# Dilated attention by units of two heads: 64-row score products, 64-column output products, the row sum folded into the head norm

## The chip, the cores and the metric

The kernel is one program on one core of a Trainium2 chip. The metric is the device time of one execution in microseconds. TensorE, VectorE, ScalarE and GpSimd each run their own list of instructions and meet through semaphores; SyncE and GpSimd issue the DMAs.

## The reference

Three model blocks follow each other on a sequence of 1024 tokens with 1024 channels, all in float32. Only the attention of the third block is touched by the change:

```python
q = rms_norm(q.reshape(B, S, 8, 64), q_norm_g) * 64 ** -0.5
k = rms_norm(k.reshape(B, S, 8, 64), k_norm_g)
for window, dilation in ((128, 1), (512, 4), (2048, 16)):
    num, m, den = dilated_band(q, k, v, slopes, window, dilation)   # softmax parts of one band, with an ALiBi bias
attn = sum(exp(m_i - max) * num_i) / sum(exp(m_i - max) * den_i)
attn = rms_norm(attn, attn_out_g.reshape(8, 64))                     # over the 64 channels of a head
```

The kernel computes the three bands as one causal attention: a key that several bands hold gets the logarithm of their count added to its bias, a key that none holds gets -1e30. So for one head the work is: scores of 1024 queries against the keys up to them, plus a bias table, row maximum, exp, row sum, product with the values, division, and an RMS norm over the head's 64 channels.

## The kernel before

Activations lie transposed: a tile is 128 channels x 1024 tokens, so one tile of `A` holds two heads, head e=0 on partitions 0 to 63 and e=1 on 64 to 127. There are four such pairs; `A[:, pair]` is q, `A[:, pair + 4]` is k, `B[:, pair]` is v. The stage lies between the linear layer `qkv3` and the linear layer `rwl`. GpSimd clears `X` and copies each head's q rows into a tile of its own with zeros in the other 64 rows (`q_staged`, L2318 to L2323), while `qkv3` still runs; with these a score product over all 128 rows gives one head's scores.

One step of the loop is one head and one block of 128 queries: 64 steps (`BLOCKS_3`), 16 for a pair, e=0 first. Within a head the blocks go 7, 0, 6, 1, 5, 2, 4, 3; block b meets b + 1 blocks of 128 keys. A float32 product is two matrix instructions, each with its own weight load; a float32 transpose is one.

For step g the engines do, each in the order given, with `g+2` the step ahead and `g-1` the one behind:

- TensorE: scores of g+2 (L2482, weights the 128 queries, moving the keys, at most 512 at a time), the b + 1 transposes of g (L2490), the output of g-1 (L2501: weights 128 keys x 128 queries of weights, moving 128 keys x 64 channels, b + 1 of them accumulated).
- VectorE: score plus bias with the row maximum out of PSUM (L3017, `tensor_tensor_reduce`, up to 1024 wide), the negation of the maximum (L3021), the copy of the transposed rows of g out of PSUM (L3028), the reciprocal of the row sum (L3030).
- ScalarE: exp of g+2 with its row sum (L2832), the copy of the output of g-1 scaled by the reciprocal (L2839).

Once a pair: two halves of v transposed into tokens x channels (TensorE L2464, ScalarE L2809); for the finished pair squares (ScalarE L2814), their sum (VectorE L2999), square root (ScalarE L2818, with a table load, and another load for the next exp), reciprocal and scaling (VectorE L3003, L3006), and the transposes back to channels x tokens (TensorE L2464, ScalarE L2822). Scores have two places in PSUM (banks 0 and 1 for the wide blocks, bank 2 for the others), the transposes two (4 and 5, and 7), the output one (bank 6). The bias tables of two heads at a time lie in `kept`, loaded by GpSimd's queue (L2327).

After the stage, `rwl` (L183) runs its 64 instructions at once, in the order of tiles and halves (0,0), (1,0), (0,1), (1,1), with the last pair's transposes between them. GpSimd then saves the attention's result (L2329) and loads `pair_const` (L2331); VectorE waits for that load (L3091) before it evacuates `rwl`'s banks (L3043, L3045), which the next layer's products wait for.

Of the kernel before, what the change touches and what calls it, by code (L numbers as in the profile page):

```python
# [18 lines left out]
P = 128  # L19
# [73 lines left out]
def build(nc, io, out):  # L93

    with ExitStack() as ctx:
# [2005 lines left out]
        if 3 in BLOCKS:  # L2101
# [4 lines left out]
            bias_landed = [sem(f"bias_landed{e}") for e in range(2)]  # L2106
# [4 lines left out]
            qk_dve = steps("qk_vector", "recip " + " ".join(f"scaled{m}" for m in range(DT)))  # L2111

            BLOCK_ORDER = [7, 0, 6, 1, 5, 2, 4, 3]
            BLOCKS_3 = [(pair, e, b) for pair in range(4) for e in range(2) for b in BLOCK_ORDER]
            NB = len(BLOCKS_3)
            VTURN_AT = {16 * (pair - 1) + at: (pair, half) for pair in range(1, 4) for half, at in ((0, 10), (1, 12))}
            OTURN_AT = {16 * (pair + 1) + at: (pair, half) for pair in range(3) for half, at in ((0, 6), (1, 8))}
            OSQ_AT, OSUM_AT, OSTD_AT, OSCALE_AT = ({16 * (pair + 1) + at: pair for pair in range(3)} for at in (1, 2, 3, 4))

            def along(first, last, extras, *kinds):  # L2120

                names = [first]
                for g in range(-2, NB + 1):
                    names += [f"{kind}{g + lag}" for kind, lag in kinds if 0 <= g + lag < NB]
                    for table, made in extras:
                        if g in table:
                            names.append(made(table[g]))
                return " ".join(names + [last])
            half_name = lambda kind: lambda at: f"{kind}{at[0]}_{at[1]}"
            named = lambda *kinds: lambda pair: " ".join(f"{kind}{pair}" for kind in kinds)  # L2130
            dil_pool = steps("dilated_gpsimd", " ".join(f"low{pair} high{pair}" for pair in range(4)))
            dil_pe = steps("dilated_tensor", along("vturn0_0 vturn0_1", "oturn3_0 oturn3_1",
                                                   [(VTURN_AT, half_name("vturn")), (OTURN_AT, half_name("oturn"))],
                                                   ("s", 2), ("turn", 0), ("o", -1)))
            dil_act = steps("dilated_scalar", along("vtok0_0 vtok0_1", "osq3 ostd3 oout3_0 oout3_1",
                                                    [(OSQ_AT, named("osq")), (OSTD_AT, named("ostd")), (VTURN_AT, half_name("vtok")),
                                                     (OTURN_AT, half_name("oout"))], ("exp", 2), ("on", -1)))
            dil_dve = steps("dilated_vector", along("", "osum3 orstd3 oscale3",
                                                    [(OSUM_AT, named("osum")), (OSCALE_AT, named("orstd", "oscale"))],
                                                    ("max", 2), ("neg", 2), ("pt", 0), ("recip", 0)))  # L2140
            dil_zero = steps("dilated_zero", "zeroed")

            q_staged = lambda pair, e: X[:, 2 * pair + e, :]
            v_heads = [C[:, 7, :].rearrange("p (s n) -> p s n", s=NT), B[:, 4, :].rearrange("p (s n) -> p s n", s=NT)]
            o_heads = [B[:, 5, :], B[:, 6, :]]
            o_room = norm_sums.rearrange("p w j t -> p (w j t)")[:, 0:SEQ]
            small_rows = C[:, 6, :].rearrange("p (n t) -> p n t", n=2)
            p_rows = lambda g: small_rows[:, g // 2 % 2, :] if g % 2 else C[:, 4 + g // 2 % 2, :]
            p_cols = lambda g: B[:, 7, 0:HALF] if g % 2 else C[:, 3, :]
            score_bank = lambda g: bank[:, 2, :] if g % 2 else pair_banks(0)  # L2150
            turn_rows = lambda g: bank[:, 7, :] if g % 2 else pair_banks(4)
            out_cols = lambda g: bank[:, 6, 0:64]
            head_sum = kept[:, 0:8 * P].rearrange("p (m r) -> p m r", m=8)
            head_spread = kept[:, 8 * P:16 * P].rearrange("p (m r) -> p m r", m=8)
            row_max, row_neg, row_sum3, row_recip3 = (cols[:, 4 * n:4 * n + 4] for n in range(4))
            o_sum, o_std, o_rstd = (cols[:, 16 * n:16 * n + 16] for n in (1, 2, 3))
# [154 lines left out]
        def b3_gpsimd(pool):  # L2311
# [4 lines left out]
            pool.memset(X[:, :, :], 0.0).then_inc(*dil_zero.did("zeroed"))  # L2316
            pool.wait_ge(*dil_zero.all())
            for pair in range(4):  # L2318
                pool.wait_ge(*qk_dve.after(0, f"scaled{pair}"))
                for e, name in enumerate(("low", "high")):  # L2320
                    rows = slice(64 * e, 64 * e + 64)
                    nc.gpsimd.tensor_copy(q_staged(pair, e)[rows], A[rows, pair, :]).then_inc(*dil_pool.did(f"{name}{pair}"))
                    pool.wait_ge(*dil_pool.after(0, f"{name}{pair}"))  # L2323
            for pair in range(4):
                for e in range(2):
                    pool.wait_ge(*(dil_dve.after(0, f"max{16 * (pair - 1) + 8 * e + 7}") if pair else qk_pe.after(0, "spread7")))
                    pool.dma_start(kept[:, e * SEQ:(e + 1) * SEQ], io["dilated_bias"][2 * pair + e]).then_inc(bias_landed[e], 16)  # L2327
# [1181 lines left out]
```

## Time and profile before

| | us |
|---|---|
| median of 3 runs | 4563.32 |
| the runs | 4549.02, 4565.37, 4563.32 |
| span of the profiled execution | 4563.6 |
| TensorE busy in it | 4427.4 (97%) |
| VectorE, ScalarE, GpSimd busy | 1772.2, 900.7, 852.0 |
| dilated stage, 2784.1 to 2989.06 | 204.96 |

The times shown don't mark which run was profiled; its span lies 0.3 us above their median, and that span is taken as its own time too. The stage is found by the first transposes of v (L2464) at 2784.14 us and the first instruction of `rwl` at 2989.06 us. Busy time of a matrix instruction includes its run through the array after its last column went in, so instructions in a row overlap in the record; the pace of a run of them is read from start to start or from the chain of waits.

### The profile page before, as it was taken

What the parts mean: (1) busy time and instruction counts of PE and PEld (TensorE: products, weight loads), DVE (VectorE), ACT (ScalarE), POOL (GpSimd) and SP (SyncE); (2) the same over time, 40 slices, a digit from 0 to 9 for tenths busy, and PEclk for the clock granted to TensorE, in tenths of its full rate; (3) what the DMA queues carried; (4) which work ended last, traced back from release to release, by engine and by line L of the source; (5) the groups of instructions that cost most, each with busy time, mean ns of one, the idle gap of its engine ahead of it and who ended that gap; (6) DMA issues with size and microseconds to landing.
All of it is one profiled execution on the core that took longest, in us unless ns stands there. A gap on an engine that the chain in (4) does not pass through costs nothing.

```text
span 4563.6 us, 37880 instructions
## 1 busy us (share of the span) xinstructions
PE 4427.4 (97%) x15188; PEld 2387.4 (52%) x15188; DVE 1772.2 (39%) x2821; ACT 900.7 (20%) x1603; POOL 852.0 (19%) x656
## 2 busy tenths in 40 slices
PE   8999999999999999999999999899999999999999
PEld 4467444444444456654444445644699744444444
DVE  4635463333325123333996403534333332222311
ACT  2114120000002122221332112431244310000000
POOL 5212042423201100000552000000111003222310
PEclk9989999999999999999999999999999999999999
DMA  4420101111111110001111111010000121111121
GB/s 188 157 82 1 37 28 37 46 46 46 37 46 65 37 72 12 10 19 37 37 37 46 56 46 37 19 49 28 14 1 1 56 92 42 41 46 46 66 75 44
DMA packets 52605, 215.45 MB, mean 47 GB/s; under 512 B 5856, under 2 KB 7392, under 8 KB 50512
## 3 DMA queue, kind: packets, MB, share of 16 engines
q1 hardware_dynamic: 47808, 168.58, 10.5%
q0 software_dynamic: 4624, 44.45, 2.5%
q8 instruction: 122, 2.00, 0.2%
q14 instruction: 51, 0.42, 0.0%
HBM read 194.13 MB, written 18.87 MB: 47 GB/s over the span
## 4 chain that ended last, share of the span: by engine, by line
PE 91%; DVE 4%; POOL 1%; ACT 1%; issue 1%; DMA 1%; SPq 0%; DVEq 0%; POOLq 0%; ACTq 0%
PE bank L474 30%; PE bank L183 28%; PE bank L2554 7%; PE bank L2741 4%; PE bank L1700 2%; PE bank L1753 2%; PE bank L2752 1%; PE bank L1736 1%; PE bank L2482 1%; PE bank L1739 1%; PE bank L2501 1%; PE bank L2581 1%; PE bank L1716 1%; PE bank L2730 1%; PE bank L2682 1%
## 5 line engine op out<-in xcount | busy, mean ns | idle before, releaser
L183 PE MATMUL bank<-H,ring 128*128 128x512 f32 x1920 | 835.2, 596 | 10.6 <-ACT H L371 4.7
L183 PEld LDWEIGHTS bank<-H,ring 128*128 128x128 f32 x1920 | 366.1, 191 | 469.9 <-issue 454.2
L183 PE MATMUL bank<-ABC,ring 128*128 128x512 f32 x1200 | 520.1, 594 | 2.5 <-POOL ABC L1654 2.0
L183 PEld LDWEIGHTS bank<-ABC,ring 128*128 128x128 f32 x1200 | 226.7, 190 | 286.4 <-issue 278.0
L474 PE MATMUL bank<-H,ring 128*128 128x512 f32 x736 | 323.5, 593 | 0.8 <-ACT ABC L1799 0.8
L2067 DVE SCALAR_TENSOR_TENSOR bank<-ABC,params,bank 128x1024 f32<-128x1024 f32 x184 | 237.3, 1290 | 8.0
L474 PEld LDWEIGHTS bank<-H,ring 128*128 128x128 f32 x736 | 140.0, 190 | 176.9 <-issue 176.9
L474 PE MATMUL bank<-H,X 128*128 128x512 f32 x400 | 179.9, 593 | 0.4 <-POOL H L825 0.4
L474 PE MATMUL bank<-X 128*128 128x512 f32 x400 | 179.8, 593 | 0.0
L474 PE MATMUL bank<-X,ring 128*128 128x512 f32 x368 | 165.4, 593 | 0.0
L1639 POOL TENSOR_TENSOR ABC<-ABC 128x1024 f32<-128x1024 f32 x48 | 113.3, 2361 | 220.4 <-ACT ABC L1873 214.4
L1186 ACT ACTIVATE norm_room<-bank 128x512 f32<-128x512 f32 x27 | 16.1, 597 | 612.7 <-PE bank L474 612.7
L474 PEld LDWEIGHTS bank<-H,X 128*128 128x128 f32 x400 | 76.0, 190 | 96.3 <-issue 94.6
L474 PEld LDWEIGHTS bank<-X 128*128 128x128 f32 x400 | 76.1, 190 | 95.5 <-issue 95.3
L474 PE MATMUL bank<-ABC,ring 128*128 128x512 f32 x288 | 126.1, 593 | 0.0
L461 POOL TENSOR_TENSOR X<-ring 128x512 f32<-128x512 f32 x31 | 39.9, 1286 | 457.2 <-DMA ring<-in_gu 185.8
L474 PEld LDWEIGHTS bank<-X,ring 128*128 128x128 f32 x368 | 70.0, 190 | 87.9 <-issue 87.9
L3151 DVE COPY_PREDICATED ring<-kept,bank 128x512 f32<-128x512 int32 x80 | 56.5, 724 | 151.9 <-PE bank L2554 151.9
L1993 DVE CUSTOM_DVE_ANT_0 H<-bank,kept 128x1024 f32<-128x1024 f32 (+3 forms) x64 | 48.3, 754 | 170.3 <-PE bank L1739 170.3
L1489 DVE SCALAR_TENSOR_TENSOR ABC<-bank,params,norm_room 128x512 f32<-128x512 f32 x60 | 45.1, 751 | 171.2 <-PE bank L474 171.2
L2345 POOL COPY X<-ABC 64x256 f32<-64x256 f32 x128 | 50.6, 396 | 294.4 <-PE bank L2581 266.1
L2554 PE MATMUL bank<-ring,H 128*128 128x128 f32 x720 | 97.9, 284 | 3.8 <-DVE H L3171 2.1
(548 smaller groups left out, 6780.8 us busy)
## 6 DMA issues: line engine op xcount, KB each, us to landing
ABC<-in_ada SPq DMA_DIRECT2D x48, 512.0 KB, 5.7
ring<-in_gu SPq DMA_DIRECT2D x44, 512.0 KB, 4.2
ring<-in_up SPq DMA_DIRECT2D x32, 512.0 KB, 4.0
ring<-in_down SPq DMA_DIRECT2D x32, 512.0 KB, 4.1
ring<-in_conv_in SPq DMA_DIRECT2D x24, 512.0 KB, 4.2
ring<-in_ffn SPq DMA_DIRECT2D x16, 704.0 KB, 5.3
ring<-in_proj SPq DMA_DIRECT2D x16, 512.0 KB, 5.9
ring<-in_mix SPq DMA_DIRECT2D x16, 512.0 KB, 4.4
```

Source lines behind the costliest of these rows:

```text
L183: mm = nc.tensor.matmul(bank[:, 2 * (m % 2) + h, :], ring[:, s % RING, k * P:(k + 1) * P], rhs(k)[:, h * HALF:(h + 1) * HALF], start=(k == ...
L474: mm = nc.tensor.matmul(S.bank(j, slot), lhs[:, k * P:(k + 1) * P], rhs[:, k, :], start=start and k == 0, stop=(k == 3), skip_group_check= ...
L1639: nc.gpsimd.tensor_tensor(C[:, c, :], C[:, c, :], conv_parts[k % 2], ALU.add).then_inc(*conv_pool.did(f"tap{k}"))
L1700: mm = nc.tensor.matmul(bank[:, b + h, :], w(first + k), A[:, src + k, h * HALF:(h + 1) * HALF], start=(k == 0), stop=(k == n - 1))
L1716: mm = nc.tensor.matmul(bank[:, 6 + c // 4, (c % 4) * P:(c % 4 + 1) * P], A[:, 3 + k, c * P:(c + 1) * P], w(5 + k), start=(k == 0), stop=( ...
L1753: mm = nc.tensor.matmul(bank[:, 6, 0:P], p_turned(n)[:, k * P:(k + 1) * P], v_tok[:, k, :], start=(k == 0), stop=(k == LENGTHS[n]))
L1993: nc.vector.tensor_tensor_reduce(p_exp(n)[:, 0:(b + 1) * P], score_bank(n)[:, 0:(b + 1) * P], causal_row[:, (NT - 1 - b) * P:], 1.0, -3e38 ...
L2067: nc.vector.scalar_tensor_tensor(conv_rows(c), conv_us[c % 4][:, k:k + SEQ], conv_tap(c, k), conv_rows(c), ALU.mult, ALU.add).then_inc(*co ...
L2345: last = nc.gpsimd.tensor_copy(dst[rows, :, block], src[rows, :, chunk3(c)])
L2554: mm = nc.tensor.matmul(bank[:, b, at + q * width:at + q * width + width], lhs[:, q, :], rhs(q), start=start and (q == 0 or stop), stop=st ...
L2741: mm = nc.tensor.matmul(bank[:, down_bank[b], :], lhs[:, k * P:(k + 1) * P], rhs[:, k, :], start=start and k == 0, stop=stop and k == 7, s ...
L3151: nc.vector.copy_predicated(x_lev[n], mask_i(n, 0), bank_q(2 if n < 3 else 3)).then_inc(*rw_dve.did(f"x{n}_{c}"))
```

## The change

The loop now goes over 32 units of one pair and one block, both heads together. Scores are two products over 64 rows each (`A[rows, ...]` with rows 0 to 63 and 64 to 127), into two banks, so GpSimd's clearing and copying of q is gone. A unit with more than four key blocks is worked in two parts of at most 512 keys. The q spread constants and the bias table are negated on the host: scores come out negated, VectorE takes a minimum with the running value of the first part, and exp runs with scale -1 and the minimum as bias, so no negation is left. The output product is turned: weights are 64 columns of v (128 keys x 64 channels), moving are the transposed rows, and the two heads write partitions 0 to 63 and 64 to 127 of one bank, channels x queries already. Nothing is divided by the row sum: with n the unscaled output and s the row sum, the norm of n/s is n / sqrt(mean(n*n) + eps*s*s). For that ScalarE squares the output of each unit, TensorE takes the mean by a product with the two columns of `one_head` (eight products of 2 columns a pair), and 16 products (weights a broadcast column, moving the identity) spread the reciprocal root back over 64 partitions each; VectorE scales. The copy of the transposed rows is split: head 0 by VectorE, head 1 by ScalarE.

In a step ScalarE does the copy of part 0 of unit g, the copy and the squares of the output of g-1, the copy of part 1, the two exps of g+2, and in the step after a pair's mean product the square root. VectorE does the variance or the reciprocal of the finished pair where due, the two minima of part 0 of g+2, the copy of part 0 of g, the minima of part 1, the copy of part 1, and the scaling where due. The reciprocal is the first thing of VectorE's step 3 behind a pair, the spread products the last of TensorE's steps 3 and 5.

```diff
@@ schedule
-            BLOCKS_3 = [(pair, e, b) for pair in range(4) for e in range(2) for b in BLOCK_ORDER]
+            UNITS = [(pair, b) for pair in range(4) for b in BLOCK_ORDER]
+            parts_of = lambda n: [(a, min((UNITS[n][1] + 1) * P, a + HALF)) for a in range(0, (UNITS[n][1] + 1) * P, HALF)]
+            behind = lambda at: {8 * (pair + 1) + at: pair for pair in range(3)}
+            MS_AT, VAR_AT, RECIP_AT, SPREAD0_AT, SCALE0_AT, SPREAD1_AT, SCALE1_AT = (behind(at) for at in (1, 2, 3, 3, 4, 5, 5))
+            VTURN_AT = {8 * (pair - 1) + 6 + half: (pair, half) for pair in range(1, 4) for half in range(2)}
+            bias_rows = [kept.rearrange("p (e t) -> p e t", e=2), C[:, 4:6, :]]
+            dilated_bank = lambda n, i, e: bank[:, 2 * ((PART_AT[n] + i) % 2) + e, :]
+            out_rows = bank[:, 7, 0:P]
+            mean_squares = bank[:, 6, 0:16]
@@ GpSimd
-            pool.memset(X[:, :, :], 0.0).then_inc(*dil_zero.did("zeroed"))
...
-                    nc.gpsimd.tensor_copy(q_staged(pair, e)[rows], A[rows, pair, :]).then_inc(*dil_pool.did(f"{name}{pair}"))
...
-            pool.wait_ge(*dil_act.all())
+            pool.wait_ge(*dil_dve.all())
             pool.dma_start(attention_kept, C[:, 0:4, :]).then_inc(mix_spilled, 16)
@@ TensorE
+            def scores(n, i):
...
+                    pe.wait_ge(*dil_dve.after(0, f"max{m}_{before - PART_AT[m]}_1"))
+                a, z = parts_of(n)[i]
+                for e in range(2):
+                    rows = slice(64 * e, 64 * e + 64)
+                    mm = nc.tensor.matmul(dilated_bank(n, i, e)[:, 0:z - a], A[rows, pair, b * P:(b + 1) * P], A[rows, pair + 4, a:z],
+                                          start=True, stop=True)
+            def rows_turned(n, i):
...
+                for e, copied in enumerate((dil_dve, dil_act)):
+                    if i == 0:
+                        pe.wait_ge(*dil_act.after(0, f"exp{n}_{e}"))
+                    if i:
+                        pe.wait_ge(*copied.after(0, f"pt{n}_{i - 1}"))
...
+                    for at in range(a, z, P):
+                        mm = nc.tensor.transpose(bank[:, 4 + e, at - a:at - a + P], p_rows(n, e)[:, at:at + P], ident[:, :])
+            def heads_out(n):
...
+                pe.wait_ge(*dil_dve.after(0, f"pt{n}_{last}"))
+                pe.wait_ge(*dil_act.after(0, f"pt{n}_{last}"))
+                if n:
+                    pe.wait_ge(*dil_act.after(0, f"square{n - 1}"))
+                for k in range(b + 1):
+                    for e in range(2):
+                        rows = slice(64 * e, 64 * e + 64)
+                        mm = nc.tensor.matmul(out_rows[rows], v_heads[pair % 2][:, k, rows], p_cols(n, e)[:, k * P:(k + 1) * P],
+                                              start=(k == 0), stop=(k == b), skip_group_check=True)
+            def heads_mean(pair):
...
+                for b in range(NT):
+                    mm = nc.tensor.matmul(mean_squares[:, 2 * b:2 * b + 2], out_squares[pair % 2][:, b * P:(b + 1) * P], one_head,
+                                          start=True, stop=True, skip_group_check=True)
+            def heads_spread(pair, half, b):
+                pe.wait_ge(*dil_dve.after(0, f"recip{pair}"))
+                for n in range(4):
+                    for e in range(2):
+                        at = 2 * (4 * half + n) + e
+                        mm = nc.tensor.matmul(bank[64 * e:64 * e + 64, b, n * P:(n + 1) * P], o_rstd[:, at:at + 1].broadcast_to([P, 64]),
+                                              ident[:, :], start=True, stop=True, skip_group_check=True)
+            for g in range(-2, NU + 1):
+                if g + 2 < NU:
+                    scores(g + 2, 0)
+                if 0 <= g < NU:
+                    rows_turned(g, 0)
+                if g + 2 < NU:
+                    scores(g + 2, 1)
+                if 0 <= g - 1:
+                    heads_out(g - 1)
+                if 0 <= g < NU:
+                    rows_turned(g, 1)
...
+            linear(pe, "rwl", lambda k: H[:, k, :], between={(1, 0, 0): lambda: heads_mean(3), (0, 1, 4): lambda: heads_spread(3, 0, 4),
+                                                            (0, 1, 5): lambda: heads_spread(3, 1, 5)})
@@ ScalarE
+                nc.scalar.activation(p_cols(n, 1)[:, a:z], bank[:, 5, 0:z - a], ACT.Identity).then_inc(*dil_act.did(f"pt{n}_{i}"))
+                nc.scalar.activation(C[:, pair, now], out_rows, ACT.Identity).then_inc(*dil_act.did(f"kept{n}"))
+                nc.scalar.activation(out_squares[pair % 2][:, now], out_rows, ACT.Square).then_inc(*dil_act.did(f"square{n}"))
+                    nc.scalar.activation(rows, rows, ACT.Exp, scale=-1.0, bias=row_min(n, e, last),
+                                         accum_out=row_sums(pair)[:, 2 * b + e:2 * b + e + 1]).then_inc(*dil_act.did(f"exp{n}_{e}"))
@@ VectorE
+                    nc.vector.tensor_tensor_reduce(p_rows(n, e)[:, a:z], dilated_bank(n, i, e)[:, 0:z - a], bias_rows[pair % 2][:, e, at + a:at + z],
+                                                   1.0, row_min(n, e, 0) if i else 3e38, ALU.add, ALU.min, row_min(n, e, i)
+                nc.vector.tensor_copy(p_cols(n, 0)[:, a:z], bank[:, 4, 0:z - a]).then_inc(*dil_dve.did(f"pt{n}_{i}"))
+                nc.vector.tensor_tensor(o_twice, row_sums(pair), row_sums(pair), ALU.mult).then_inc(*dil_dve.did(f"twice{pair}"))
+                nc.vector.scalar_tensor_tensor(o_twice, o_twice, eps_rms, mean_squares, ALU.mult, ALU.add).then_inc(*dil_dve.did(f"var{pair}"))
+                v.wait_ge(*dil_act.after(0, f"std{pair}"))
+                nc.vector.reciprocal(o_rstd, o_std).then_inc(*dil_dve.did(f"recip{pair}"))
+                nc.vector.scalar_tensor_tensor(rows, rows, par("attn_out_g", pair), bank[:, b, :], ALU.mult, ALU.mult
@@ host
-                head_const[2 * m + e, 8 + m, rows] = 0.125 if m < 4 else 1.0
+                head_const[2 * m + e, 8 + m, rows] = -0.125 if m < 4 else 1.0
-        arrays["dilated_bias"] = bias.astype(np.float32)
+        arrays["dilated_bias"] = (-bias).astype(np.float32)
```

## Rows read from the trace of the kernel before

**Rows 1.** Busy time by engine: the dilated stage, then its second pair.

```profile
core 0: us, PE busy (x) PEld busy (x) DVE busy (x) ACT busy (x) POOL busy (x), PEclk, DMA share, GB/s
...
2784.10:2989.06 204.96, 182.84 (x1112) 138.98 (x1113) 112.36 (x329) 90.90 (x220) 3.17 (x6) 0.94 0.07 21
...
2836.00:2887.00 51.00, 45.79 (x280) 34.63 (x279) 28.65 (x83) 23.48 (x56) 1.05 (x2) 0.93 0.07 21
```

**Rows 2.** Waits in 2785 to 3000 us: waiter, releaser, total us, times, longest.

```profile
DVE ABC L3017 <- PE bank L2482: 105.5, 35, 22.9
ACT ABC L2832 <- DVE cols L3021: 90.0, 47, 4.7
```

**Rows 3.** Chain that ended last, pieces in the stage: start, us, what.

```profile
2825.95 0.65 PE bank L2490 x6
...
2829.92 1.79 PE bank L2482 x4
...
2836.34 3.10 PE bank L2482 x4
...
2842.22 1.97 PE bank L2501 x16
...
2850.55 1.28 ACT L2818
```

**Rows 4.** Groups by line and form, 2780 to 3010 us: TensorE's products.

```profile
L2501 PE MATMUL bank<-ABC 128*128 128x64 f32 x576 | 74.4, 275 | 20.3 <-ACT ABC L2839 17.1 <-DVE cols L3030 1.4 <-DVE ABC L3028 1.1
...
L2482 PE MATMUL bank<-ABC,X 128*128 128x512 f32 x96 | 58.0, 706 | 1.3 <-DVE cols L3017 1.3
```

**Rows 5.** The same view: VectorE and ScalarE, widest and narrowest forms.

```profile
L2839 ACT ACTIVATE ABC<-bank,cols 128x64 f32<-128x64 f32 x64 | 19.3, 302 | 22.9 <-PE bank L2501 22.9
...
L3017 DVE CUSTOM_DVE_ANT_0 ABC<-bank,kept 128x1024 f32<-128x1024 f32 x8 | 9.8, 1225 | 43.4 <-PE bank L2482 43.4
...
L3028 DVE COPY ABC<-bank 128x1024 f32<-128x1024 f32 x8 | 9.8, 1224 | 0.0
...
L2832 ACT ACTIVATE ABC<-ABC,cols 128x1024 f32<-128x1024 f32 x8 | 9.2, 1148 | 27.2 <-DVE cols L3021 27.2
...
L2809 ACT ACTIVATE ABC<-bank 128x512 f32<-128x512 f32 x8 | 4.6, 586 | 0.8 <-PE bank L2464 0.8
...
L2832 ACT ACTIVATE ABC<-ABC,cols 128x128 f32<-128x128 f32 x8 | 3.1, 391 | 0.0
L3028 DVE COPY ABC<-bank 128x128 f32<-128x128 f32 x8 | 2.3, 291 | 0.0
L3017 DVE CUSTOM_DVE_ANT_0 ABC<-bank,kept 128x128 f32<-128x128 f32 x8 | 2.2, 273 | 0.0
```

**Rows 6.** Timeline of TensorE in an earlier stage: start, us, line, tile*form.

```profile
380.50 1.02 PE L964 MATMUL bank<-kept,ident 128*128 128x512 f32 x2
381.45 1.16 PE L967 MATMUL bank<-ABC,kept 64*128 64x128 f32 x8
382.44 0.61 PE L972 MATMUL bank<-ABC,kept 64*128 64x128 f32 x4
382.98 0.66 PE L977 MATMUL bank<-ident,ABC 128*128 128x128 f32 x4
```

**Rows 7.** Windows of 2 us within the stage, columns as Rows 1.

```profile
2834.00:2836.00 2.00, 1.12 (x10) 1.15 (x10) 1.11 (x7) 1.12 (x5) 0.00 (x0) 0.97 0.00 0
2836.00:2838.00 2.00, 2.00 (x5) 0.96 (x5) 0.00 (x0) 0.31 (x1) 0.00 (x0) 0.50 0.00 0
```

**Rows 8.** Timeline after the stage: start, us, engine, line, idle before.

```profile
2989.06 15.67 PE L183 MATMUL bank<-H,ring 128*128 128x512 f32 x32 [0.45 <-ACT ABC L2839]
...
3010.59 0.53 POOL L2331 DMA_DIRECT2D kept<-in_pair_const  x1
...
3019.03 0.88 DVE L3091 TENSOR_SCALAR ring<-kept,params 128x128 f32<-128x128 f32 x4 [24.58 <-DMA kept<-in_pair_const]
...
3021.43 8.82 PE L183 MATMUL bank<-H,ring 128*128 128x512 f32 x20 [2.09 <-DVE ABC L3045]
```

More of the change, by code:

```diff
@@ L2117, in build @@
[L2117 to L2134, printed above, removed]
@@ new lines, in part, with unit, extra @@
+            def part(kind, lag, i, *ends):
+                return lambda g: [f"{kind}{g + lag}_{i}{end}" for end in ends or ("",) if 0 <= g + lag < NU and i < len(parts_of(g + lag))]
+            def unit(lag, *kinds):
+                return lambda g: [kind.format(g + lag) for kind in kinds if 0 <= g + lag < NU]
+            def extra(table, *kinds):
+                return lambda g: [kind.format(table[g]) for kind in kinds if g in table]
+            turned_v = lambda g: [f"vturn{VTURN_AT[g][0]}_{VTURN_AT[g][1]}"] if g in VTURN_AT else []
@@ new lines, in heads_spread @@
+            def heads_spread(pair, half, b):
[5 more added lines that the diff above has]
+                                              ident[:, :], start=True, stop=True, skip_group_check=True)
+                mm.then_inc(*dil_pe.did(f"spread{pair}_{half}"))
@@ L2514, in b3_tensor @@
-            pe.wait_ge(*last_in_bank3)
-            pe.wait_ge(*dil_act.after(0, f"on{NB - 1}"))
-            linear(pe, "rwl", lambda k: H[:, k, :], between={(0, 1, 0): lambda: out_turned(3, 0, 4), (0, 1, 4): lambda: out_turned(3, 1, 5)})
+                    if half:
+                        pe.wait_ge(*dil_act.after(0, f"vtok{pair}_0"))
+                    elif pair >= 2:
+                        pe.wait_ge(*dil_dve.after(0, f"scale{pair - 2}_1"))
+                    else:
+                        pe.wait_ge(*dil_act.after(0, "vtok0_0"))
@@ new lines, in weights @@
+            def weights(n):
+                pair, b = UNITS[n]
+                last = len(parts_of(n)) - 1
+                if n % 8 == 0 and pair >= 2:
+                    act.wait_ge(*dil_dve.after(0, f"var{pair - 2}"))
+                for e in range(2):
+                    act.wait_ge(*dil_dve.after(0, f"max{n}_{last}_{e}"))
+                    rows = p_rows(n, e)[:, 0:(b + 1) * P]
+                    nc.scalar.activation(rows, rows, ACT.Exp, scale=-1.0, bias=row_min(n, e, last),
+                                         accum_out=row_sums(pair)[:, 2 * b + e:2 * b + e + 1]).then_inc(*dil_act.did(f"exp{n}_{e}"))
```

297 lines of the change are left out of this document (144 added, 153 removed).

## Prediction

> **What bounds the kernel now.** The busy table first: TensorE is busy in 4427 of 4563.6 us and everything else under 40%, so only what shortens or lengthens TensorE's own line counts. The change touches one stage, so the next view is the windows. The stage takes 204.96 us; TensorE is busy in 182.84 of them (89%), VectorE in 112.36, ScalarE in 90.90, at a granted clock of 0.94 [rows 1]. A pair of heads takes 51 us. It is the least dense part around: 22 us of TensorE idle, and about 12% of the stage at 1.2 GHz (a mean of 0.94 between 0.5 and 1.0), which costs up to another 12 us. The waits say that VectorE and ScalarE are not behind by load: VectorE waits 105.5 us for scores, ScalarE 90.0 us for maxima [rows 2]. The chain runs through scores and outputs with short pieces of the others between, so it is TensorE's work plus the latency of a round trip where a wide block meets a narrow one.
>
> TensorE's paces at full clock, from the chain [rows 3]: six transposes in 0.65 us, 0.108 each; a wide block's scores, 8 key blocks in four instructions, 1.79 us, so 0.224 for a key block of one head; sixteen output instructions of 64 columns in 1.97 us, 0.123 each, so 0.246 for a key block. An output instruction moves half the columns of a transpose and is no faster: its weight load sets the pace. The counts are 576 output and 192 score instructions [rows 4], two for each product. A pair has 72 key blocks (2 heads x 36): scores 16.1, transposes 7.8, outputs 17.7, v and results turned 16 x 0.108 = 1.7; together 43.3 us, 173 for four pairs. The other 32 us of the stage are the idle and the slow clock above.
>
> **TensorE after.** *Scores.* The columns and the two instructions a product stay, so one behind the other they cost the same 16.1 us. Whether the two heads' products can run in the array together is the question of the change, and no row shows it: the only 64-row products of the trace (an earlier stage) all use the same rows, and run one behind the other, eight in 0.99 us [rows 6]. The bounds: no overlap, 4 passes for two heads; and overlap. Each product is two instructions on the same half of the array, issued in order, so the order is low, low, high, high: the first high one can go beside the second low one, and 3 passes are left of 4 for a part that stands alone. That is 12.1 us. The kernel gives the two products disjoint rows, disjoint operands and different banks, so nothing in the program ties them. I take the overlap. The Trainium skill (TensorEngine Tiling (Array Packing), Key Properties) states that different tiles can execute weight loads and products in parallel; no run here shows it yet.
>
> *Outputs.* Turned, each moves 128 columns under a weight load of 64 columns. The pace of one is between a transpose's 0.108 and the 0.123 of today; 0.115 taken. One behind the other: 144 x 0.115 = 16.6 us a pair, 1 less than now. With overlap of the two halves of columns, the run of a unit has 2(b+1)+1 passes, 80 for a pair's eight units, 9.2 us. *Per pair:* transposes of the weights as before 7.8, of v 0.9, the results' transposes gone; mean product 16 x 0.123 = 2.0; spreads 32 x 0.115 = 3.7, with overlap 18 x 0.115 = 2.1.
>
> *Changes of tile.* Before, every instruction of the stage used the full array; now scores use 64-row tiles, outputs and spreads 64-column ones, transposes and the mean the full one. A wide step changes tile 5 times, a narrow one 3 times, 32 a pair and 2 for the extras: 34. What one costs is in the earlier stage [rows 6]: 380.50 to 381.45 holds two 512-column passes (2 x 0.43 = 0.86), 0.09 over; 382.44 to 382.98 holds four of 0.108 and goes back to the full array, 0.11 over. So 0.1 each, 3.4 us a pair. The skill's page names this as a rule against such a mix (same section: a change of mode drains TensorE). The row agrees that it costs, at 0.1 us; a costlier one is the last rival. For 64-column tiles there is no row: from 0.1 to 0.35 us (0.275 - 0.108 = 0.17 for the run-out of the record [rows 4], and some 0.19 for a weight load no longer hidden).
>
> Sum of a pair: with overlap 12.1 + 7.8 + 9.2 + 0.9 + 2.0 + 2.1 + 3.4 = 37.5 us; without 16.1 + 7.8 + 16.6 + 0.9 + 2.0 + 3.7 + 3.4 = 50.5. The last pair's mean and spreads lie behind the stage: 4 x 37.5 - 4.1 = 146 against 4 x 50.5 - 5.7 = 196, where now it is 173 of work.
>
> **The other engines.** From the widest and narrowest of eight forms [rows 5], a cost is linear in the width: the masked maximum 0.137 + 0.136 per 128 columns, the copy 0.158 + 0.133, the exp 0.283 + 0.108, ScalarE's copy out of PSUM about 0.26 + 0.08 (0.302 at 64, 0.586 at 512). *VectorE* a pair: minima as before 12.0 plus 8 second parts of 0.137 = 13.2; their accumulator reads 24 x 0.08 = 2.0; half the copies 6.1 + 4 x 0.158 = 6.7; the pair's extras about 2.2: 24 us, against 28.65 now (no negation, no reciprocal by unit, no reduction). *ScalarE:* exps 12.4 as before; copies of transposed rows, new, 12 parts, 12 x 0.26 + 36 x 0.08 = 6.0; output copy and square 16 x 0.34 = 5.4 in place of 16 x 0.302; v 1.2; root and two table loads of 1.28 [rows 3] 2.9: 28 us, against 23.5 now. Both are below 37.5, so they hide, but ScalarE is at three quarters and its order is fixed.
>
> So I follow one wide step with the next narrow one, from the step's start on TensorE, unit 7 at g, 6 at g+2, with overlap. TensorE: scores part 0 to 1.4, transposes 2.3, scores part 1 3.4, output of the unit behind 4.5, transposes 5.4; narrow step: scores 6.1, transposes 6.4, the wide output from 6.4. VectorE: minima to 3.0, copy 3.7, minima 5.0, copy 5.8. ScalarE: copy 3.0, output and squares 5.2, copy 6.1, exps 8.3. The wide output needs both copies (6.1: ready), the next wide step's transposes the exps at 8.3 (they come at 9.8: ready). The round trip that stalls TensorE now is covered by the score parts and transposes, with margins of some tenths. I allow 1.5 us a pair for missed ones.
>
> Once a pair it fails: VectorE's reciprocal heads step 3 and waits for the root, which ScalarE does behind the exps of step 2 and a table load. By the same count the minima of step 2 end at 4.8, exps 6.9, root 8.5, reciprocal 8.8, while TensorE reaches the spreads at 7.5; VectorE's minima of step 3, queued behind the reciprocal, come 3 us late. 2 us, three times: 6. The fill (two score parts, four minima, two exps before the first transpose) leaves TensorE idle 3 us, the last unit's chain 3 us, and I keep 2 us of slow clock at the fill; with fuller work I expect no other fall.
>
> **Ahead and behind.** GpSimd's clearing and copying lay beside `qkv3`: nothing gained. Bias loads keep a pair of tables ahead: nothing. Behind the stage, `rwl`'s products hide the last pair's work, but GpSimd's load of `pair_const` starts when that is done: now issued at 3010.59, 21.5 us into `rwl`, landed at 3019.03, and TensorE resumes at 3021.43 after a wait of 2.09 [rows 8]. After: mean products at 6.9 us, first spread at 19.2 (24 passes of 0.43, plus 2.0 and changes), second to 22.4, scaling 23.3, issue 24.1 instead of 21.5: TensorE resumes 2.6 us later, a new cost on the path; 4 us without overlap.
>
> **The sum**, against the execution profiled (4563.6 us, 0.3 above the median shown): stage 146 + 6 + 6 + 3 + 3 + 2 = 166, so -39; behind it +2.6; total -36.5: **4527 us**.
>
> **The rivals.**
> *Overlap for one kind only.* If the outputs gain nothing (four weight loads a key block set a pace, as they do now), the stage is 180 of work and 14 of waits: -11 + 4, 4557 us. If only the outputs overlap: 162 + 18, -25 + 2.6, 4541. For it: today's outputs run at their weight load's pace. Chance 0.17.
> *No overlap, cheap changes.* The 64-row products of the earlier stage, one behind the other, speak for it as far as they go. 196 of work; TensorE is then so full that 10 us of waits do: +1.5, tail +4: 4569 us. All that the turned outputs and the denser line win goes into spreads, means and changes. Chance 0.13.
> *Slower.* The narrow tiles without overlap, and a change to or from a 64-column tile at 0.35 instead of 0.1: 136 changes x 0.25 = 34 us more, 4603 us; from 0.3 us a change on it is over the bound for slower by itself. With overlap the same price gives 4561. A second road to the same side is the clock: it fell to 0.50 behind 2 us in which TensorE was busy 1.12 [rows 7], and four score instructions then took 3.10 us against 1.79 [rows 3]; with 146 us of work, half the stage at 1.2 GHz costs 50 us or more. Against it, idle shrinks. Chance 0.15.
> *The forecast*, overlap of both, chance 0.55; its own range 4508 (no waits beyond fill, and passes at 0.108) to 4543 (ScalarE in the way).
>
> Measurement can't tell less than about 0.5% (23 us) from no change. Below 4540.5: nine tenths of the forecast's case and part of the one-kind case, 0.58; within: the rest of these and the no-overlap case, 0.27; above 4586: 0.15. The range 4508 to 4569 leaves out the slower rival and little else.
>
> **What would show it.** In the timeline, high-row products starting one pass behind the second low one (or four passes in a row); a unit's outputs at 2(b+1)+1 passes; 0.1 us between tiles; a pair at about 40 us; VectorE's reciprocal waiting for ScalarE some 3 us, three times; `pair_const` issued 24 us into `rwl`. A pair at 50 us with TensorE over 95% busy would say no overlap; a granted clock below 0.9, the clock.

## The result, and the profile after

The changed kernel takes 4497.54 us (median of 4 runs, 4494.57 to 4502.98) against 4558.19 for the kernel before (4 runs, 4549.02 to 4565.37): a ratio of 0.9867, 95% interval 0.9849 to 0.9884, or 60.6 us less. The forecast was 4527 us with a range from 4508 to 4569: the direction was right, but the time lies below the range, and the gain was 1.7 times the 36.5 us forecast.

The stage, from the first transposes of v to the first instruction of `rwl`, in the windows view of the kernel after:

```profile
core 0: us, PE busy (x) PEld busy (x) DVE busy (x) ACT busy (x) POOL busy (x), PEclk, DMA share, GB/s
2779.65:2918.33 138.68, 132.43 (x1233) 90.46 (x1233) 80.19 (x255) 97.05 (x256) 2.10 (x4) 1.00 0.07 24
```

Against [rows 1]: 204.92 us have become 138.68, so 66.2 less. TensorE's idle went from 22.1 to 6.2, the granted clock from 0.94 to 1.00. What TensorE is busy with shrank by 50.4, and part of that is the clock. By the paces of [rows 3] the work before was 173 us at full clock; 205 - 173 - 22 leaves some 10 us for the slow clock. That is a remainder. Added up over windows of 0.5 us in the same stretch, the granted clock below 1.0 cost 11.9 us before and nothing after. So the gain divides into some 40 us of work, 16 of idle and 10 to 12 of clock.

TensorE's groups after, by line and form (busy, mean ns, idle before):

```profile
L2490 PE MATMUL bank<-ident,X 128*128 128x128 f32 x288 | 42.4, 282 | 0.7 <-ACT X L2860 0.4 <-DVE X L3069 0.3
...
L2474 PE MATMUL bank<-ABC 64*128 64x512 f32 x96 | 26.8, 639 | 0.8 <-DVE cols L3060 0.8
L2505 PE MATMUL bank<-X,ABC 128*64 128x128 f32 x416 | 26.2, 276 | 0.0
```

The 96 widest score instructions are still 96, and a single one takes about as long as a 512-column pass elsewhere (639 ns mean, 593 to 596 in the linear layers before), yet together they occupy 26.8 us where they occupied 58.0 [rows 4], some slow clock in it. Durations that stay while the busy time halves mean that two run at once. The timeline shows it for one part:

```profile
2792.15 1.13 PE L2474 MATMUL bank<-ABC 64*128 64x512 f32 x4
2793.21 0.33 PE L2490 MATMUL bank<-ident,X 128*128 128x128 f32 x1
```

Two heads with two instructions each, 512 columns wide: start to start 1.06 us, where four passes of 0.43 would be 1.72 and the three of the forecast 1.29. Two passes and 0.2 us are left. Two narrow windows show the order. In the first, 2792.40 to 2792.60 us, two of the four are in the array, counted from the same 2792.15; in the second, 2792.90 to 2793.10, the other two, from 2792.68:

```profile
2792.15 0.70 PE L2474 MATMUL bank<-ABC 64*128 64x512 f32 x2
...
2792.68 0.60 PE L2474 MATMUL bank<-ABC 64*128 64x512 f32 x2
```

As near as the view tells, two start together and the other two together half a microsecond later. So head 1's first instruction does not wait for head 0's second. The chain through the second half of a pair (start, us, what) gives every group's share:

```profile
2846.22 0.42 PE bank L2474 x4
2846.64 1.02 PE bank L2490 x8
2847.67 1.24 PE bank L2505 x20
...
2849.55 1.06 PE bank L2474 x4
2850.61 1.02 PE bank L2490 x8
2851.64 0.85 PE bank L2474 x4
2852.48 1.02 PE bank L2505 x16
```

Twenty output instructions in 1.24 us, sixteen in 1.02: the four more cost 0.22, so two of them go abreast every 0.11 us and 0.15 are left over for the change of tile. Before, sixteen narrower ones took 1.97 [rows 3]. Eight transposes take 1.02 instead of 0.86: again 0.15 for the change. A pair takes 35.2 us (one pair's first scores start at 2824.26, the next one's at 2859.48). TensorE's timeline has eight idle places in the stage: three in the fill (0.69, 0.85, 0.30), one behind each of the first three pairs (1.12, 1.11, 1.12), two at the end (0.37, 0.64). The first of the three behind a pair, with the chain that leads to it (exps, table load, root) and TensorE's own line:

```profile
2828.74 1.83 ACT X L2879 x4
...
2830.59 1.28 ACT L2884
...
2831.88 0.23 ACT cols L2884
...
2832.44 1.09 PE L2525 MATMUL bank<-ident,cols 128*64 128x128 f32 x16 [1.12 <-DVE cols L3080]
```

and behind the stage, over all engines:

```profile
2941.74 0.54 POOL L2326 DMA_DIRECT2D attention_kept<-ABC  x1 [100.72 <-DVE ABC L3085]
2942.27 0.53 POOL L2327 DMA_DIRECT2D kept<-in_pair_const  x1
...
2950.76 0.87 DVE L3163 TENSOR_SCALAR ring<-kept,params 128x128 f32<-128x128 f32 x4 [8.07 <-DMA kept<-in_pair_const]
...
2953.16 2.52 PE L183 MATMUL bank<-H,ring 128*128 128x512 f32 x4 [2.86 <-DVE ABC L3117]
```

`pair_const` is issued 23.9 us into `rwl` (21.5 before, [rows 8]) and TensorE resumes 34.8 us into it (32.4 before). Stage and tail together: -66.2 + 2.5 = -63.7. The spans differ by 70.8. Of the other 7 us, 4.5 lie ahead of the stage, which began anywhere between 2779.5 and 2784.3 us in the runs below, whatever the kernel, and 2.5 behind the tail: from `rwl`'s first instruction to the end both kernels take 1574.5 us, so the 2.5 us of the tail do not show at the end of these two.

The two traces are not of middling runs. A run's time is some 1.8 us longer than its span. So the profiled execution of the kernel before (span 4563.6) is the run of 4565.37 us, the slowest of its four, and not one at the median as was taken above, and that of the changed kernel is the run of 4494.57, the fastest. That is why the spans differ by 70.8 us and the medians by 60.6. Among 12 more executions of the kernel before, the fastest (4549.34 us) had a granted clock of 0.991 and the slowest (4565.47) one of 0.987.

### The profile page after: what moved, and what is told of

The parts are those of the page before. It is cut to its first block, busy times and chain, and to the rows that moved or that the text cites. A ratio compares the mean times of both kernels' runs of the same rounds, so it can differ in the third digit from the quotient of the medians.

```text
span 4492.8 us, 37952 instructions
## 1 busy us (share of the span) xinstructions
PE 4374.3 (97%) x15348; PEld 2334.3 (52%) x15348; DVE 1739.7 (39%) x2750; ACT 905.1 (20%) x1639; POOL 837.1 (19%) x647
## 4 chain that ended last, share of the span: by engine, by line
PE 93%; DVE 3%; POOL 1%; ACT 1%; issue 1%; DMA 1%; SPq 0%; DVEq 0%; POOLq 0%; ACTq 0%
PE bank L474 31%; PE bank L183 29%; PE bank L2597 7%; PE bank L2784 4%; PE bank L1700 2%; PE bank L1753 2%; PE bank L2795 1%; PE bank L1736 1%; PE bank L1739 1%; PE bank L2624 1%; PE bank L2490 1%; PE bank L2474 1%; PE bank L2505 1%; PE bank L1716 1%; PE bank L2773 1%
## 5 line engine op out<-in xcount | busy, mean ns | idle before, releaser
L474 PE MATMUL bank<-H,ABC 128*128 128x512 f32 x224 | 100.7, 592 | 0.0
```

Source lines behind the costliest of these rows:

```text
L474: mm = nc.tensor.matmul(S.bank(j, slot), lhs[:, k * P:(k + 1) * P], rhs[:, k, :], start=start and k == 0, stop=(k == 3), skip_group_check= ...
```

## The experiments

The theory after the comparison: the two heads' products go abreast (at the same time on the two halves of the array), pass beside pass, because each half takes its instructions on its own; that is the surplus over the forecast. The rivals: it is the clock, or the idle time, or the cheaper form of a product by itself. Stage is in all of them the same stretch as above.

**Both score products on one tile.**

```diff
-                    mm = nc.tensor.matmul(dilated_bank(n, i, e)[:, 0:z - a], A[rows, pair, b * P:(b + 1) * P], A[rows, pair + 4, a:z],
+                    mm = nc.tensor.matmul(dilated_bank(n, i, e)[:, 0:z - a], A[0:64, pair, b * P:(b + 1) * P], A[0:64, pair + 4, a:z],
```

> The changed kernel, with the score products of both heads taken from rows 0 to 63 (so head 1 computes head 0's scores again). Counts, shapes, tiles' size and waits stay; only the second tile of the array is no longer used for scores. If the surplus over the forecast came from the two heads' passes going abreast (2 passes left of 4), a part costs 4 passes again: 36 key blocks x 2 x 0.107 = 7.7 us more a pair, less up to 1.1 us of idle, so the stage goes from 139 to 166 to 170 us and the time up by 27 to 31 us. If it came from waits and clock instead and the scores overlapped by one pass in four as forecast, the scores lose 1 pass of 4: +4 us a pair, stage near 155. If nothing of the scores' overlap is on the path: no change.

Measured: 4549.42 us, ratio 0.9976 (0.9966 to 0.9986). Most of the gain is gone, and the stage of 188.56 us is 19 to 22 us longer than expected. The windows over the stage and over some stretches in it:

```profile
2784.26:2972.82 188.56, 186.57 (x1233) 122.17 (x1233) 81.19 (x255) 98.26 (x256) 2.09 (x4) 0.86 0.05 18
...
2843.00:2845.00 2.00, 2.00 (x22) 1.83 (x18) 0.00 (x0) 1.42 (x6) 0.00 (x0) 1.00 0.00 0
2845.00:2847.00 2.00, 2.00 (x6) 0.79 (x6) 0.40 (x2) 0.00 (x0) 0.00 (x0) 0.81 0.03 8
2847.00:2849.00 2.00, 2.00 (x7) 1.23 (x7) 1.12 (x3) 0.00 (x0) 0.00 (x0) 0.50 0.00 0
```

In the chain, a part at full clock, and what came ahead of the fall at 2846 us:

```profile
2843.33 1.88 PE bank L2516 x16
2845.20 2.64 PE bank L2474 x4
...
2861.37 1.91 PE bank L2474 x4
...
2861.30 0.69 PE L2474 MATMUL bank<-ABC 64*128 64x512 f32 x1
```

At full clock the four instructions of a part take 1.91 us, against 1.06: that is the four passes. The last line is TensorE's timeline from 2861.40 to 2861.70: here one instruction is in the array 0.1 to 0.4 us after the start, where the changed kernel has two. But four times in the stage the clock fell to 0.50 for some 13 us; added up over windows of 0.5 us that is 27 us lost. The first fall came behind an idle place of 0.99 us. The other three came without any gap, 1.0 to 1.5 us behind a pair's 16 mean instructions (L2516), which move two columns each. The overlap is shown, but its price is mixed with a second thing.

**Both score products over the full array.**

```diff
-                    mm = nc.tensor.matmul(dilated_bank(n, i, e)[:, 0:z - a], A[rows, pair, b * P:(b + 1) * P], A[rows, pair + 4, a:z],
+                    mm = nc.tensor.matmul(dilated_bank(n, i, e)[:, 0:z - a], A[:, pair, b * P:(b + 1) * P], A[:, pair + 4, a:z],
```

> The changed kernel with each score product over all 128 rows (the sum of both heads' scores, twice). Against the run with both products on rows 0 to 63, which took 188.5 us for the stage at a granted clock of 0.86: the passes are the same four. Theory, that run paid twice, once for the passes (some 28 us) and once for a clock that fell while only half of the array's rows worked (some 21 us): here the clock stays above 0.97 and the stage takes 165 to 170 us. Rival, that four passes one behind the other lower the clock or stall for another reason: stage near 188 again.

```profile
2784.01:2940.41 156.40, 151.09 (x1232) 107.88 (x1233) 80.31 (x255) 97.47 (x256) 2.10 (x4) 1.00 0.07 21
...
2790.06 1.98 PE L2474 MATMUL bank<-ABC 128*128 128x512 f32 x4 [0.99 <-DVE cols L3060]
```

4518.59 us, ratio 0.9913 (0.9898 to 0.9928). The same four passes (a part takes 1.72 to 1.93 us in the chain), and the clock at 1.00 throughout, behind the same idle place of 0.99 us and the same mean products: so neither the passes nor these pulled it down by themselves. The stage is 9 to 14 us below what was expected, since the expectation forgot that scores and transposes now share a tile: 16 changes a pair are gone, 0.15 us each, 10 us. The run with one tile keeps those 10 us; the other 22 of the 32 us between the two runs are left for the clock, whose 27 us are partly made up by 3.3 us less idle. The two runs also differ in those 16 changes of tile, but the changed kernel has them too, at a clock of 1.00.

**Both output products on one tile.**

```diff
-                        mm = nc.tensor.matmul(out_rows[rows], v_heads[pair % 2][:, k, rows], p_cols(n, e)[:, k * P:(k + 1) * P],
+                        mm = nc.tensor.matmul(bank[0:64, 7, e * P:(e + 1) * P], v_heads[pair % 2][:, k, rows], p_cols(n, e)[:, k * P:(k + 1) * P],
```

> The changed kernel, with the output products of both heads written to partitions 0 to 63 (head 1 beside head 0 in the bank, so half of the output is not the attention's). 64-column weight loads, counts and waits stay; only the second tile is unused. Abreast theory: a unit's outputs take 4(b+1) passes instead of 2(b+1), 72 x 0.109 = 7.8 us more a pair, stage 167 to 170 us, time up by 28 to 31 us. Rival, that turning the product and halving its weight load made it cheap and the tiles give little: a 64-column load of half the time would let four instructions run in less than 0.43 us a key block; stage below 155.

4530.68 us, ratio 0.9938 (0.9924 to 0.9953), stage 166.68 us: +28.0, where the abreast theory said 28 to 31. (TensorE is busy 31.4 us more, and 3.4 of idle went.) A unit of 32 outputs takes 3.64 us in the chain, 0.109 each, against 0.123 in the old form [rows 3]: for 144 of them that is 2 us a pair, about what the changes of tile around them cost. The clock held but for one fall of some 4 us, again just behind a pair's mean products; it cost 1.7 us.

**The outputs head by head.**

```diff
-                for k in range(b + 1):
-                    for e in range(2):
-                        rows = slice(64 * e, 64 * e + 64)
+                for e in range(2):
+                    rows = slice(64 * e, 64 * e + 64)
+                    for k in range(b + 1):
```

> The changed kernel with a unit's output products issued head by head (all key blocks of head 0, then all of head 1) instead of in turn. Same instructions, same tiles. Theory A, each tile of the array takes its instructions from a queue of its own and may run ahead of the other by up to a unit's 16: nothing changes, stage 139 us. Theory B, instructions start in the order of the program and overlap only with their neighbours in it: the two heads' runs overlap only at the seam, +7 us a pair, stage 165 us or more. In between: a queue of limited depth, so the narrow units stay abreast and the wide ones do not.

4511.54 us, ratio 0.9900 (0.9885 to 0.9914), stage 156.03: +17.3, between the theories. The chain of waits in this run:

```profile
2812.71 1.07 PE bank L2505 x12
...
2816.03 1.95 PE bank L2505 x20
...
2821.49 1.51 PE bank L2505 x16
```

and further on, eight instructions in 0.59 and 32 in 3.28. In the changed kernel the same groups take 0.59 for 8, 0.81 for 12, 1.02 for 16, 1.24 for 20 and 1.90 for 32. Eight lose nothing: the fifth instruction, of the second head, starts beside the first, past three in its way. Twelve lose 0.26 us (2.4 passes of 0.109), sixteen 0.49 (4.5), 32 1.38 (12.7): always half the group less some three and a half. So the second tile's instructions pass waiting ones of the first, three to four deep; the depth is worked out from these times and not seen by itself. Issued in turn, as the change does, groups up to the longest here, 32, stay abreast. This run too has one fall of the clock behind mean products, for 4 us.

**64-row scores in the kernel before.**

```diff
-                        mm = nc.tensor.matmul(score_bank(n)[:, a:z], q_staged(pair, e)[:, b * P:(b + 1) * P], A[:, pair + 4, a:z],
+                        mm = nc.tensor.matmul(score_bank(n)[:, a:z], A[64 * e:64 * e + 64, pair, b * P:(b + 1) * P], A[64 * e:64 * e + 64, pair + 4, a:z],
```

> The kernel before with one part of the change alone: each score product reads its head's 64 rows of q and k instead of the zero-padded copy over 128 rows. The two heads are 8 steps apart there, so no two score products of different tiles are neighbours. Theory: 64-row products by themselves save nothing, and each of the 64 steps now changes tile twice, at 0.15 to 0.2 us each: 19 to 26 us more work for TensorE, of which some falls into its 22 us of idle: the stage from 205 to 210 to 225 us. Rival, that a 64-row product is cheaper by itself: the stage below 205.

4611.76 us, ratio 1.0116 (1.0101 to 1.0131): slower by 52 us, far beyond the expectation. The windows, and the instructions ahead of one fall of the clock:

```profile
2782.47:3038.33 255.86, 247.00 (x1112) 176.04 (x1113) 114.56 (x329) 93.30 (x220) 3.17 (x6) 0.75 0.05 17
...
2886.00:2900.00 14.00, 14.00 (x53) 10.79 (x51) 4.18 (x12) 3.11 (x8) 0.00 (x0) 0.50 0.00 0
...
2938.38 1.52 PE L2501 MATMUL bank<-ABC 128*128 128x64 f32 x12 [0.85 <-ACT ABC L2839]
2939.83 3.05 PE L2482 MATMUL bank<-ABC 64*128 64x512 f32 x4
```

Half of the stage runs at 1.2 GHz, in four stretches of 58, 28, 27 and 17 us. Each begins within 2.5 us behind an idle place (1.30 us, then three times 0.85) and goes on although TensorE is then busy without a gap. In the kernel before the clock also falls, seven times in the stage, each time within 2 us behind an idle place of 1.1 to 1.4 us, but it is back within 4 us. Added up over windows of 0.5 us, the slow clock costs 65 us here and 11.9 there. With 13 us less idle, that leaves 11 us of the 51 for the 128 changes of tile, 0.09 each and less than expected. One part of the change alone is thus the largest loss of the study: with the heads 8 steps apart nothing goes abreast, half the array rests in each score product, and the clock, once down, stays down for long. The forecast's second road to the slower side is thus a real one, though in another kernel than the one it was forecast for.

**The load of `pair_const` early.** Four edits that aim at what is left. The first moves the load ahead of the result's save, behind `max23_0_1`, the last use of that place.

```diff
+  pool.wait_ge(*dil_dve.after(0, "max23_0_1"))
+  pool.dma_start(kept[:, 0:9 * P], io["pair_const"]).then_inc(rwkv_landed, 16)
   pool.wait_ge(*dil_dve.all())
   pool.dma_start(attention_kept, C[:, 0:4, :]).then_inc(mix_spilled, 16)
-  pool.dma_start(kept[:, 0:9 * P], io["pair_const"]).then_inc(rwkv_landed, 16)
```

> The changed kernel with the load of pair_const issued as soon as the third pair's minima are done, ahead of the save of the result. Forecast's account of the tail: TensorE resumed 34.8 us after the first instruction of rwl, behind a wait of 2.86 us for VectorE, which waited 8.1 us for this load. Theory: the wait of 2.86 us goes and TensorE runs through; the next wait, 3.6 us for the weights of the next layer, is set by the ring's slots and stays or grows by what the first gives: gain 0 to 3 us, under what the times can tell, read from the trace.

4495.38 us, ratio 0.9862 (0.9847 to 0.9877), not told apart by time. In the trace TensorE no longer waits in `rwl`, and from `rwl`'s first instruction to the end it is 1571.0 us (4491.8 - 2920.8) instead of 1574.5. The three later runs with the early load have 1571.0 to 1571.4, and those of the changed kernel's form without it 1574.3 to 1578.5, so 3 us or more are the load's.

**The root's chain a step later** (with the early load).

```diff
-            MS_AT, VAR_AT, RECIP_AT, SPREAD0_AT, SCALE0_AT, SPREAD1_AT, SCALE1_AT = (behind(at) for at in (1, 2, 3, 3, 4, 5, 5))
-            VTURN_AT = {8 * (pair - 1) + 6 + half: (pair, half) for pair in range(1, 4) for half in range(2)}
+            MS_AT, VAR_AT, RECIP_AT, SPREAD0_AT, SCALE0_AT, SPREAD1_AT, SCALE1_AT = (behind(at) for at in (1, 2, 4, 4, 5, 6, 6))
+            VTURN_AT = {8 * (pair - 1) + 7 + half: (pair, half) for pair in range(1, 4) for half in range(2)}
```

> The same and the root's steps moved one step later (reciprocal and first spread in step 4 behind a pair, second spread in step 6, the turning of v in steps 7 and 8). In the trace after TensorE is idle 1.1 us before the first spread of each of three pairs, waiting for the root behind exps and table load. Theory: these 3.4 us go, nothing comes in their place; stage 138.6 to 135 to 136 us. Rival: the later steps make the bank of v and spreads the next wait, stage unchanged.

4502.27 us, ratio 0.9884 (0.9866 to 0.9903), stage 145.04: the rival. TensorE's timeline:

```profile
2827.11 1.97 PE L2506 MATMUL bank<-X,ABC 128*64 128x128 f32 x32 [1.87 <-ACT ABC L2853]
2842.55 0.44 PE L2491 MATMUL bank<-ident,X 128*128 128x128 f32 x2 [1.02 <-ACT X L2861]
```

The first output of a pair waits 1.87 us for v, which was turned a step too late, and a narrow unit's transposes wait 1.02 us for a copy; both come three times.

**The same with a wide unit's score parts together.**

```diff
                 if g + 2 < NU:
                     scores(g + 2, 0)
+                if g + 2 < NU:
+                    scores(g + 2, 1)
                 if 0 <= g < NU:
                     rows_turned(g, 0)
-                if g + 2 < NU:
-                    scores(g + 2, 1)
```

> The same and both score parts of a wide unit issued together ahead of the transposes. Saves one change of tile in 16 wide steps (0.15 to 0.2 us each) and, if instructions of the second part slip in beside the first, the 0.1 us gap between the passes: stage 3 to 5 us shorter than with the two edits alone, 131 to 133. Rival: the transposes come 0.9 us later and VectorE's copy with them, so the minima of part 1 stall it: stage the same or longer.

4500.53 us, ratio 0.9873 (0.9858 to 0.9888), stage 145.32 against 145.04. TensorE is busy 1.5 us less and idle 1.7 us more, so nothing is gained. Not all of that is the rival's. At the end of one of the idle places of 1.87 us the clock was down, for some 4 us:

```profile
2859.03 3.59 PE L2506 MATMUL bank<-X,ABC 128*64 128x128 f32 x32 [1.87 <-ACT ABC L2853]
```

The same group takes 1.97 us elsewhere. Without that fall TensorE's work is some 3 us shorter, as the theory said, and half of it is eaten by idle for VectorE's copies, as the rival said.

**The root ahead of the exps** (with the early load, the rest as changed).

```diff
+  if g in VAR_AT:
+      out_std(VAR_AT[g])
   if g + 2 < NU:
       weights(g + 2)
-  if g in VAR_AT:
-      out_std(VAR_AT[g])
```

> The changed kernel with pair_const loaded early and with ScalarE's root ahead of the two exps of its step instead of behind them; the order of all other steps as in the changed kernel. Moving the root's whole chain a step later made the stage 6.4 us longer, because the turning of v moved with it and the first output of a pair waited for v. Theory: here nothing else moves; the root is ready some 2 us earlier, the exps 1.5 us later with more than that to spare; TensorE's idle of 1.1 us before the first spread goes three times: stage 138.7 to 135 to 136 us. Rival: the exps are late for the next wide unit's transposes and the stage stays at 138 or grows. With the early load the time should be 3 to 6 us under the changed kernel's, 4489 to 4495.

> The changed kernel, nothing edited, as the base for the one beside it and for how far the same program's spans scatter: stage 138 to 139.5 us; the stage's start between 2779 and 2785 us, as in the runs so far; time 4490 to 4503.

4492.33 us (5 runs, 4490.79 to 4492.69), ratio 0.9849 (0.9835 to 0.9863). The changed kernel beside it on the same chip: 4497.42 (4 runs, 4496.27 to 4500.74), ratio 0.9862 (0.9848 to 0.9876), stage 138.59. So 5.1 us less; the runs of the two don't touch, though the intervals against the kernel before overlap. The stage takes 135.65 us, and TensorE's idle places in it up to 2860 us are:

```profile
2786.10 0.49 PE L2475 MATMUL bank<-ABC 64*128 64x128 f32 x4 [0.69 <-DVE cols L3061]
2787.44 1.13 PE L2475 MATMUL bank<-ABC 64*128 64x512 f32 x4 [0.85 <-DVE cols L3061]
2792.64 0.42 PE L2491 MATMUL bank<-ident,X 128*128 128x128 f32 x2 [0.31 <-DVE X L3070]
```

All in the fill. Beyond 2860 us only the two at the end are left (0.37, 0.64), so the 1.1 us behind each pair are gone, and stage and time are as expected. From `rwl`'s first instruction to the end it takes 1571.0 us, 3.5 less than the run beside it: the 5.1 us come from the root and the early load together. This version beats both kernels.

## Why the prediction was wrong in size

*The step that failed* is the one on the passes: "Each product is two instructions on the same half of the array, issued in order, so the order is low, low, high, high: the first high one can go beside the second low one, and 3 passes are left of 4". The timeline of one part shows two instructions starting together and the other two together one pass later, 1.06 us in all for the 1.29 of three passes, and the run head by head shows that a tile can run three to four instructions ahead of the other. Two passes are left of four. In the pair's sum, scores were put at 12.1 us without their tile changes and are 7.7 (36 key blocks x 2 x 0.107); the outputs at 9.2 and are 7.9 (72 x 0.109). With the spreads that is 6 us a pair, 24 in the stage.

*The changes of tile* were put at 0.1 us and cost 0.15 to 0.2: 0.15 on entering transposes or outputs, 0.2 for a score part with its two weight loads. That is 2.6 us a pair back, 10 in the stage, so the work came to 132.4 instead of 146. The bounds given for a change to or from a 64-column tile, 0.1 to 0.35 us, held. What the Trainium skill (TensorEngine Tiling (Array Packing), Key Properties) states of tiles in parallel is borne out by these runs (1.06 us against 1.91). That a change of mode drains the engine, as the same section states, is in line with the 0.15 to 0.2 us; that it is a drain which costs them no run shows.

*The waits* were mis-sized: 18 us of idle and 2 of slow clock allowed, 6.2 and none found. The walk through a wide and a narrow step gave no stall with "margins of some tenths"; the trace has none either, and the 1.5 us a pair put on top were not there. The once-a-pair wait for the root was found where it was forecast, in step 3 behind exps and table load (root's end 8.5 us into the step pair by the forecast; VectorE's reciprocal waits 3.6 us at its longest), but it costs TensorE 1.12 us. The walk itself gave 1.3 (8.8 - 7.5), and 2 was taken because VectorE's minima come late behind the reciprocal; that lateness cost TensorE nothing. Fill and end took 2.9 us instead of 6.

Sum: 166 - 24 for the passes + 10 for the changes of tile - 14 of waits = 138; the stage measured 138.7. The misses have different signs, so the stage came out nearer to the forecast than its passes and waits did.

*What held:* VectorE and ScalarE hidden (80 and 97 us busy of 139, so 20 and 24 a pair for 24 and 28 forecast, ScalarE the nearer); nothing from GpSimd's removed work beyond the scatter of the stage's start; the tail later by 2.5 us for 2.6 forecast, `pair_const` issued 23.9 us into `rwl` for 24.1.

*The rivals.* No overlap, and one kind only, are excluded by the runs with one tile. The slower rival's costly changes of 64-column tiles are bounded by the 0.15 us seen. Its second road, the clock, was real but did not open here. The forecast held it off with "idle shrinks". That fits the kernel before, where every fall in the stage comes behind idle, but it is only half of the reason: the run with scores on one tile has less idle (2.0 us) than the changed kernel (6.2) and a clock of 0.86. There the score products use half of the array and have no partner. The forecast did not think of that, so that the road stayed shut was in part luck.

What stays open: the stage before has nine idle places of 1.1 to 1.4 us, and its seven falls of the clock come behind seven of them. Whether its outputs, which move only 64 columns each, are needed for a fall as well was not tried.

## What to carry to other kernels

Two small products on disjoint halves of the array cost one plus the change of tile, in float32 too, if they stand next to each other in the program. Issued in turn they stayed abreast over all 32 instructions of the longest group here; issued one head after the other they lose it beyond three or four. A 64-row score product without its partner was worse than a zero-padded full one in both kernels tried: it saved nothing and kept the clock down. A 64-column output without its partner saved nothing and cost little clock. Count each change of tile at 0.15 to 0.2 us. When a walk through the queues gives no stall, an allowance for unseen ones needs a reason: here it was 6 us too much.

## What the runs showed of the hardware that was not expected

The granted clock does not follow busy time alone. With 64-row score products without partners in the changed kernel's order it was 0.86 over the stage, with TensorE idle for 2.0 us of it: three times it fell to 0.50 without a gap, just behind a pair's mean products, and stayed there for some 13 us. With one tile unused for the outputs, or with the outputs head by head, one such fall each was over after 4 us (0.99 over the stage). With 64-row score products in the kernel before it was 0.75: the falls came behind idle of 0.85 to 1.30 us, but lasted 17 to 58 us of nearly full work, where the kernel before was back within 4. With the same number of passes over all 128 rows it stayed at 1.00, and so it did with two 64-row products abreast. So with lone half-array score products the clock fell behind mean products where it otherwise mostly held, and each time it stayed down several times as long. No run varies the rows in use and nothing else: the two runs with four passes also differ in their changes of tile, which the changed kernel has as well, at 1.00.
